# Turned modulation product, a projection that opens tile by tile, and other PSUM banks for attention's output

## The reference

```python
shift, scale, gate = jnp.split(jax.nn.silu(c) @ ada_w[l] + ada_b[l], 3, axis=-1)
shift_c, scale_c, gate_c = jnp.split(jax.nn.silu(c_ctx) @ ada_w[l] + ada_b[l], 3, axis=-1)
u = rms_norm(x, norm_w[l]) * (1.0 + scale[:, None, :]) + shift[:, None, :]
uc = rms_norm(ctx, norm_w[l]) * (1.0 + scale_c) + shift_c
rkv, ga, lw, la, q, k, v, gr, ma, mb = split_cols(u @ w_in[l])
...
# second block: causal attention with two softmaxes per head
a = p[:, :, 0] - lam * p[:, :, 1]
return jnp.einsum('bhqk,bhkv->bhqv', a.astype(vt.dtype), vt)
...
attn = rms_norm_2(attn, subln_w[l]) * (1.0 - lambda_init)
```

## Time and profile before

| | us |
|---|---|
| median of 3 runs | 5221.07 |
| profiled execution | 5224.11 |
| its span | 5222.3 |
| TensorE busy | 4907.5 (94%) |
| VectorE busy | 2560.6 (49%) |
| ScalarE busy | 1869.5 (36%) |
| GpSimd busy | 438.1 (8%) |
| mean granted clock of TensorE, share of 2.4 GHz | 0.959 |

### The profile page before, as it was taken

The page is one execution under the profiler, slowest core; times in us unless marked ns, Lnnn a source line. Parts: engine busy times, 40 slices in busy tenths (PEclk is TensorE's granted clock), DMA queues, the critical chain, the costliest instruction groups (busy, mean ns, idle before and its releaser), DMA issues. The chain is left out here.

```text
span 5222.3 us, 69250 instructions
## 1 busy us (share of the span) xinstructions
PE 4907.5 (94%) x29122; PEld 3966.2 (76%) x29122; DVE 2560.6 (49%) x3695; ACT 1869.5 (36%) x3141; POOL 438.1 (8%) x352
## 2 busy tenths in 40 slices
PE   8999999999989999999999779789999869999999
PEld 7878777778878888888888634367778547888777
DVE  2144545446434555555455367444543655555543
ACT  2133434345334554545455323311233653111111
POOL 0000000000012222232222100000000000000000
PEclk6999999999989999999999889889999879999999
DMA  4234333334221011011100153242220021212222
GB/s 174 86 131 146 130 137 140 131 140 148 104 104 44 13 49 52 13 57 44 57 13 1 50 157 116 73 139 96 97 76 30 17 89 65 73 73 73 81 93 89
DMA packets 149364, 444.05 MB, mean 85 GB/s; under 512 B 16432, under 2 KB 46256, under 8 KB 131776
## 3 DMA queue, kind: packets, MB, share of 16 engines
q1 hardware_dynamic: 133712, 385.03, 21.0%
q0 software_dynamic: 9584, 33.63, 1.8%
q10 hardware_dynamic: 5760, 20.97, 1.1%
HBM read 295.91 MB, written 142.61 MB: 84 GB/s over the span
## 5 line engine op out<-in xcount | busy, mean ns | idle before, releaser
L167 PE MATMUL pr_ps<-uhl,w_split 128*128 128x512 f32 (+1 forms) x1520 | 589.3, 388 | 0.7 <-PEq L198 0.7
L171 PE MATMUL pr_ps<-uhl,w_split 128*128 128x512 f32 (+1 forms) x1520 | 572.8, 377 | 0.0
L170 PE MATMUL pr_ps<-uhl,w_split 128*128 128x512 f32 (+1 forms) x1520 | 572.5, 377 | 0.0
L1349 DVE TENSOR_TENSOR b_G<-b_ps,cst 128x512 fp32r<-128x512 f32 x480 | 328.4, 691 | 335.5 <-PE b_ps L1150 334.2
L132 ACT ACTIVATE w_split<-w_ring 128x2048 fp32r<-128x2048 f32 x112 | 214.1, 1911 | 750.5 <-DVE ou_vc L2962 271.2
L167 PEld LDWEIGHTS pr_ps<-uhl,w_split 128*128 128x128 f32 x1520 | 288.3, 190 | 79.7 <-issue 29.3
L170 PEld LDWEIGHTS pr_ps<-uhl,w_split 128*128 128x128 f32 x1520 | 288.2, 190 | 56.9 <-issue 6.3
L171 PEld LDWEIGHTS pr_ps<-uhl,w_split 128*128 128x128 f32 x1520 | 287.9, 189 | 53.2
L1030 ACT ACTIVATE b_X<-b_ps 128x512 fp32r<-128x512 f32 x400 | 240.0, 600 | 242.0 <-PE b_ps L1150 242.0
L1150 PE MATMUL b_ps<-b_G,b_Y 128*128 128x128 f32 x1920 | 313.3, 286 | 13.5 <-DVE b_G L1349 13.1
L1034 ACT ACTIVATE b_Y<-b_ps 128x512 fp32r<-128x512 f32 x480 | 286.6, 597 | 88.6 <-PE b_ps L1150 88.6
(11 more groups left out here) (444 smaller groups left out, 10156.5 us busy)
## 6 DMA issues: line engine op xcount, KB each, us to landing
w_ring<-in_w_in SPq DMA_DIRECT2D x49, 1024.0 KB, 5.2
proj<-pr_stage SPq DMA_DIRECT2D x160, 256.0 KB, 2.0
w_ring<-in_w_up SPq DMA_DIRECT2D x24, 1024.0 KB, 4.7
ar<-pr_AR SPq DMA_DIRECT2D x32, 512.0 KB, 2.7
b_AR<-ar SPq DMA_DIRECT2D x16, 1024.0 KB, 8.8
pr_raw<-proj SPq DMA_DIRECT2D x48, 256.5 KB, 3.5
ada<-in_ada_w SPq DMA_DIRECT2D x24, 512.0 KB, 3.5
ff<-ou_vc ACTq DMA_DIRECT2D x24, 512.0 KB, 2.6
```

The costliest lines, as they stand in the source:

```text
L167: mm = nc.tensor.matmul(dst, a[0], b[0], start=start, stop=False)
L170: nc.tensor.matmul(dst, a[0], b[1], start=False, stop=False)
L171: return nc.tensor.matmul(dst, a[1], b[0], start=False, stop=stop)
L1349: L[x]["dve"].done(V.tensor_tensor(Gs[x][:], heads(x, 0), rep(K(f"lev{m}"), 4), ALU.mult), f"{n}.G{m}")
```

## The change

- The modulation product is turned: `cond` is the stationary operand, padded with zeros from 2 to 32 columns, and the weights are the moving one. Two matmuls of 512 columns per slab (column groups 0 and 1, or 2 and 3, by turns) for the first 16 slabs, four of 256 columns (groups 0 to 3) for the last 8. ScalarE copies the resulting rows out of PSUM (`line`), TensorE turns them with 4 and 2 transposes, and VectorE adds the bias. `ada_w` is laid out by rows; a slab stays 512 KB.
- Each square is done in two halves of 640 tokens in four banks.
- Weight chunk 1 is loaded behind all slabs and the constants, and the identity matrix ahead of the slabs; the others of the constants are waited for in `project`.
- The first block ends with three tiles of `uhl` made (`CUT_EARLY`); the other five are made at the start of `project`. The first six jobs become `opening`, which loops over k outside and over the jobs inside, and waits for each tile of `uhl`.
- `project` allocates the same tensors in another order, so that the ones over the old place of `u` are written late.
- In attention, heads 0 and 1 are flipped at t = 0 of heads 2 and 3, head 2 at the end before the last product, through banks 1 and 3; head 3 last, through banks 4 and 5. `end` is two instructions. `gates` waits for `head_out`.

The diff, cut:

```diff
+CUT_EARLY = 3
...
+class Modulate:
...
+    def scale(self, k):
+        for a, lo, hi in ((0, 0, T), (1, T, TA)):
+            ins = self.nc.vector.tensor_scalar(self.u[:, k, lo:hi], self.u[:, k, lo:hi], self.mod[:, 8 + k, a:a + 1],
+                                               self.mod[:, k, a:a + 1], ALU.mult, ALU.add)
+        ins.then_inc(self.ready, 1)
+
+    def hi(self, act, k):
+        act.wait_ge(self.ready, k + 1)
+        self.cut.hi(self.hl, k, self.u[:, k])
+
+    def lo(self, dve, k, base):
+        dve.wait_ge(self.cut.hi_ready, base + k + 1)
+        self.nc.vector.tensor_tensor(self.hl[1][:, k], self.u[:, k], self.hl[0][:, k].bitcast(F32), ALU.subtract).then_inc(self.cut.lo_ready, 1)
...
+    MS, MT, CA, SP, SQ = 16, 24, 2 * HALF, TA // 2, TA // 4
...
-        cond = sb("cond", [P, KT, 2])
...
+        cond = sb("cond", [P, KT, 32])
...
-        aw = sb("ada", [P, NA, KT, P])
-        ps = ctx.enter_context(nc.psum_tensor("ps_norm", [P, 4, HALF], F32))
+        aw = sb("ada", [P, NA, CA])
+        line = sb("ada_row", [P, 3 * CH])
+        ps = ctx.enter_context(nc.psum_tensor("ps_norm", [P, 8, HALF], F32))
@@ -205,14 +231,14 @@
                 sp.dma_start(par[:], G["par_dram"]).then_inc(par_in, 16)
                 for k in range(KT):
                     sp.dma_start(u[:, k], xT[:, k]).then_inc(x_in[k], 16)
+                sp.dma_start(ident, G["cst_dram"][:, CST["ident"] * P:(CST["ident"] + 1) * P]).then_inc(ident_in, 16)
                 for m in range(MS):
                     load_ada(m)
-                for l in range(NBUF):
-                    ring.load(sp, w_first[l], 0, 0, l, split=True)
+                ring.load(sp, w_first[0], 0, 0, 0, split=True)
                 for m in range(MS, MT):
                     load_ada(m)
-                sp.dma_start(G["cst"][:], G["cst_dram"]).then_inc(cst_in, 16)
-                sp.wait_ge(cst_in, 16)
+                sp.dma_start(cst[:, P:], G["cst_dram"][:, P:]).then_inc(G["cst_in"], 16)
+                ring.load(sp, w_first[1], 0, 0, 1, split=True)
 
@@ -224,19 +250,23 @@
...
-                    if k:
-                        act.wait_ge(sq_summed, k)
-                    nc.scalar.activation(sq[:], u[:, k], ACT.Square).then_inc(sq_ready, 1)
-                act.wait_ge(sq_summed, KT)
+                    for h in range(2):
+                        if k:
+                            act.wait_ge(sq_summed, 2 * k + h - 1)
+                        nc.scalar.activation(sq[:, h * SP:(h + 1) * SP], u[:, k, h * SP:(h + 1) * SP], ACT.Square).then_inc(sq_ready, 1)
+                act.wait_ge(sq_summed, 2 * KT)
...
+                act.wait_ge(ada_used, MS)
+                nc.scalar.activation(line[:, 0:HALF], ps[:, 4], ACT.Copy).then_inc(line_out, 1)
                 ring.split_first(act, True)
-                for k in range(KT):
-                    act.wait_ge(u_ready, 2 * k + 2)
-                    cut.hi([uhl[:, 0], uhl[:, 1]], k, u[:, k])
+                for k in range(CUT_EARLY):
+                    mdl.hi(act, k)
+                act.wait_ge(ada_used, MT)
+                nc.scalar.activation(line[:, HALF:], ps[:, 5, 0:CH], ACT.Copy).then_inc(line_out, 1)
@@ -244,65 +274,71 @@
...
-                    pe.wait_ge(sq_ready, k + 1)
-                    for c in range(3):
-                        w = min(HALF, TA - c * HALF)
-                        mm = nc.tensor.matmul(ps[:, c, 0:w], ones[:], sq[:, c * HALF:c * HALF + w],
-                                              start=k == 0, stop=k == KT - 1)
-                    mm.then_inc(sq_summed, 1)
-                pe.wait_ge(cond_ready, 1)
...
-                for m in range(MT):
+                    for h in range(2):
+                        pe.wait_ge(sq_ready, 2 * k + h + 1)
+                        for b in (2 * h, 2 * h + 1):
+                            mm = nc.tensor.matmul(ps[:, b, 0:SQ], ones[:], sq[:, b * SQ:(b + 1) * SQ], start=k == 0, stop=k == KT - 1)
+                        mm.then_inc(sq_summed, 1)
+                pe.wait_ge(cond_ready, 2)
+
+                def ada(m, bank, groups, w, k):
                     pe.wait_ge(ada_in[m % NA], 16 * (m // NA + 1))
-                    for k in range(KT):
-                        mm = nc.tensor.matmul(ps[:, 3, 2 * m:2 * m + 2], aw[:, m % NA, k], cond[:, k, :], start=k == 0, stop=k == KT - 1)
+                    for n, g in enumerate(groups):
+                        mm = nc.tensor.matmul(ps[32 * g:32 * g + 32, bank, 0:w], cond[:, k], aw[:, m % NA, n * w:(n + 1) * w], start=k == 0, stop=k == KT - 1)
                     mm.then_inc(ada_used, 1)
-                    if m == MS - 1:
-                        pe.wait_ge(u_ready, 1)
+
+                def turn(tiles, bank, at, n):
+                    pe.wait_ge(line_out, n)
+                    for j in range(tiles):
+                        mm = nc.tensor.transpose(ps[:, bank, j * P:(j + 1) * P], line[:, at + j * P:at + (j + 1) * P], ident)
+                    mm.then_inc(turned, 1)
+                for m in range(MS):
+                    ada(m, 4, (0, 1) if m % 2 == 0 else (2, 3), HALF, m // 2)
+                pe.wait_ge(ident_in, 16)
+                turn(4, 6, 0, 1)
+                for m in range(MS, MT):
+                    ada(m, 5, range(4), CH, m - MS)
+                turn(2, 7, HALF, 2)
...
+                nc.vector.memset(cond[:], 0.0).then_inc(cond_ready, 1)
...
-                ring.split_first(dve, False)
...
-                def row(m0, m1):
+                def row(m0, tiles, bank, n):
+                    m1 = m0 + 4 * tiles
+                    dve.wait_ge(turned, n)
...
+                row(0, 4, 6, 1)
...
-
-                def modulate(k):
-                    for a, lo, hi in ((0, 0, T), (1, T, TA)):
-                        nc.vector.tensor_scalar(u[:, k, lo:hi], u[:, k, lo:hi], mod[:, 8 + k, a:a + 1],
-                                                mod[:, k, a:a + 1], ALU.mult, ALU.add).then_inc(u_ready, 1)
-                modulate(0)
-                for k in range(KT):
-                    if k + 1 < KT:
-                        modulate(k + 1)
-                    cut.lo(dve, [uhl[:, 0], uhl[:, 1]], k, u[:, k])
-                dve.wait_ge(ada_used, MT)
-                row(MS, MT)
+                mdl.scale(0)
+                ring.split_first(dve, False)
+                for k in range(CUT_EARLY):
+                    mdl.scale(k + 1)
+                    mdl.lo(dve, k, 0)
+                row(MS, 2, 7, 2)
                 s.wait()
-                cut.wait(dve, KT)
-        cut.base += KT
+        G["cut"].base += KT
@@ -486,6 +523,7 @@
 
             @block.gpsimd
             def _(pool):
+                mdl.cut.wait(pool, 0)
@@ -506,6 +544,17 @@
...
+                def opening():
+                    for k in range(KT):
+                        mdl.cut.wait(pe, k + 1 - KT)
+                        for j in range(NB):
+                            l, m, c, w = jobs[j]
+                            rows = slice(m * P, (m + 1) * P)
+                            mm = product3(nc, ps[:, j, 0:w], [h[:, k, rows] for h in hl], [uhl[:, e, k, c:c + w] for e in range(2)],
+                                          k == 0, k == KT - 1, begun if j == 0 and k == 0 else None)
+                            if k == KT - 1:
+                                mm.then_inc(made, 1)
@@ -522,6 +571,7 @@
...
+                            pe.wait_ge(G["cst_in"], 16)
...
-                    dense(j)
+                    if j == 0:
+                        opening()
+                    elif j >= NB:
+                        dense(j)
@@ -628,6 +681,8 @@
...
+                for k in range(CUT_EARLY, KT):
+                    mdl.hi(act, k)
@@ -747,6 +802,11 @@
...
+                for k in range(CUT_EARLY, KT):
+                    if k + 1 < KT:
+                        mdl.scale(k + 1)
+                    mdl.lo(dve, k, mdl.cut.base - KT)
+                dve.wait_ge(G["cst_in"], 16)
@@ -2305,6 +2365,7 @@
...
+        flat_at = lambda h, x: ps[:, 4 + x] if h + 1 == A_HEADS else ps[:, 1 + 2 * x]
@@ -2349,8 +2410,6 @@
...
-                    if t == 5 and h:
-                        pe.wait_ge(head_out, h)
@@ -2369,6 +2428,8 @@
                 def gates(k, x):
                     if x == 0:
                         pe.wait_ge(conv, k + 1)
+                        if k >= 2:
+                            pe.wait_ge(head_out, k - 1)
@@ -2382,7 +2443,7 @@
                 def flip(h):
                     pe.wait_ge(scaled, h + 1)
                     for t in range(8):
-                        mm = nc.tensor.transpose(TR[:, t * P:(t + 1) * P], raw[:, h % 2, t], K("ident"))
+                        mm = nc.tensor.transpose(flat_at(h, t // 4)[:, t % 4 * P:(t % 4 + 1) * P], raw[:, h % 2, t], K("ident"))
@@ -2391,15 +2452,17 @@
...
-                    if t == 6 and h:
-                        pe.wait_ge(aT_ready, n - 1)
-                        flip(h - 1)
```

(24 more changed lines are left out.)

32 lines of the change are left out of this document (18 added, 14 removed).

## The result

The changed kernel takes **5162.5 us** (median of 4 runs, 5158.6 to 5163.6); the kernel before, timed beside it, 5221.9 us (5217.6 to 5230.3, 4 runs). The ratio is 0.9883, with a 95% interval of 0.9866 to 0.9900: 59 us or 1.2% faster. The forecast was 5150 with a range of 5132 to 5175. The profiled execution has a span of 5159.7 us (before: 5222.3), 62.6 us shorter.

A forecast was written before the change was run, and what follows sets the result against it. The prediction took TensorE to bound the span nearly everywhere; 54.3 us from the first stage plus 16.5 from attention make 70.8 off the median 5221.1, so 5150 us, range 5132 to 5175.

The forecast's parts named there:

- The squares: First stage: half squares of 640 columns make TensorE the bound; end moves from 38.1 to near 27.0 us.
- "low clock" of the first tile: First stage, squares: the first tile stays at 4.61 us, put down to a low clock.
- The price of a slab: Modulation product: column groups run side by side; 1.00 us of TensorE per early slab, at most 0.5 to 1.0 per late.
- The rivals that live from TensorE as the bound: Modulation product costs TensorE more than transfers: opening at 70 to 162, time 5158 to 5250; chances 0.13, 0.07, 0.04, 0.03.
- (b): Modulation product: column groups don't run side by side, at the high clock; opening at 77, time 5165; chance 0.07.
- (a): Modulation product: clock stays low while slabs stream, 2.0 us each; opening at about 70, time 5158; chance 0.13.
- The pace of the slabs: Modulation product: weights pace it at 1.35 us per slab, bounds 1.26 and 1.6; projection opens at about 62.0.
- The new wait before job 6: End of the projection's opening: TensorE waits 2.2 us, as ScalarE and VectorE split chunk 1 after job 0.
- First stage: Up to the projection's job 6: opening 56.5 us earlier less a new wait of 2.2, giving 54.3 us.
- Attention: Attention: other banks remove three waits for ScalarE's evacuation; net 18.8 - 0.6 - 1.9 = 16.3, taken as 16.5 us.
- The 5.8 for the clock in head 2: Attention, unit 7 to next unit 0: long wait lowered the clock; distance falls from 12.30 to 6.47, gaining 5.8 us.
- What is late next is VectorE's `p` for unit 5: Attention: with the three waits for ScalarE gone, VectorE's `p` comes next; unit 6 to 7 takes head 0's 10.94 us.

## Why the prediction was right, and where not

**The squares** were forecast to end at 27.0 and ended at 26.0. Right; what is late next was hidden, as said. The forecast's "low clock" of the first tile was an inference from 4.61 us where the other tiles take 2.42: the granted clock reads 1.00 from 6 to 12 us, so what slowed that tile isn't shown.

**The price of a slab** was 1.00 us of TensorE from a row with two groups. A slab alone took 1.05, so this was right; only where four lay ready and shared four groups were they 0.48 each. The rivals that live from TensorE as the bound fall. One group, the condition of (b), opened the projection at 69.0, not 77: a column cost 0.86 ns (0.44 us for 512) and not 0.95, and three of the slabs kept their groups. The clock was low for parts of this stage (0.83 and 0.66 in two of the stretches), as (a) feared. The fifth and sixth slab took 3.21 us together for that, and even then TensorE waited for the next one, so at most a little of the pace is due to it.

**The pace of the slabs** is the term that failed. Forecast were 1.35 us, a fifth slab at 31.6, the twenty-fourth used at 60.2. The fifth came at 30.65, but from there to the last it was 33.1 us for 19 slabs and the chunk: with 2.5 for the chunk, 1.61 us a slab, the forecast's upper bound. The round trip was put together from a landing time of 3.5 us of a lone slab; with four under way the median is 5.3. The forecast treated the 415 GB/s and the round trip as two limits of which the larger counts; with four buffers each cost some. The projection opened at 66.95 instead of 62.0; that the fifth slab came 0.9 us early was lost again behind the last one. And the pause from 22 to 28 us was in the forecast's own words, "four slabs are in place when the squares end", without the step that the queue stands still meanwhile. The run with ten buffers shows both.

**The new wait before job 6** was forecast at 2.2 us and measured 2.2 (2.17). The rounds of the opening waited for nothing and took 3.48 us, the first, at the low clock, 5.62. First stage: 49.3 instead of 54.3, the whole miss being the pace.

**Attention**: the mechanism held and half the sum did not. From unit 6 to 7, 4.78 + 4.78 + 3.45 = 13.0 were forecast; measured are 4.2 + 4.2 + 4.45 = 12.9. The 5.8 for the clock in head 2 were not won (12.10 from unit 7 to the next 0, where 12.30 stood), and head 1 lost 5.3 there (12.30 for 7.03). The step that failed is the argument that the long wait had brought the clock down and a short one would not. In head 1 the clock fell inside the new wait of 3.9 us, where behind the old one of 7.3 it was soon back. In head 2 it fell before the wait had begun. With the waits filled it fell in neither. The 8.1 us measured are 12.9 less 5.3, plus and minus small terms. "What is late next is VectorE's `p` for unit 5" was right, and the row of what VectorE itself was waiting for there, which the forecast did not read, held another 23 us, the clock's share included.

**The unchanged stages** were taken as unchanged. In the profiled pair they gave 5.3 us (55.9 less 49.3 before attention, then 1.3 lost), which brings the span to -62.6. That part is luck. It is no effect of the change. The mixing stage, with the same instructions, takes 642.1 us before, 636.6 after, and 642.1 in the second run of the kernel after. The mean clock was 0.98, 0.99 and 0.98. The row of the kernel before (columns as in the earlier trace rows):

```profile
3409.00:4051.10 642.10, 624.38 (x2775) 495.94 (x2776) 288.54 (x300) 160.47 (x142) 24.57 (x49) 0.98 0.24 82
```

The row of the kernel after in its second run:

```profile
3360.40:4002.50 642.10, 624.39 (x2775) 495.82 (x2776) 288.55 (x300) 160.48 (x142) 24.57 (x49) 0.98 0.24 82
```

Without it, 49.3 + 8.1 = 57.4, and the medians say 59.

So the time was inside the range and 12.5 us above the forecast: 5.0 from the slabs' pace, 8.4 from attention, less what the unchanged stages happened to give (5.3 us in the profiled pair, some 2 in the medians).

## What to carry to other kernels

When a wait goes, read on the engine that is late next not only how long it works but what it waits for itself: in attention a step of 1.2 us, queued ahead of what TensorE needed, held more than the banks did. A stream through few buffers pays twice, once while the consumer is busy elsewhere and once because each landing takes longer than alone; memory that is written only later can lend the buffers. A stage in which nothing was edited can differ by 5 us from one kernel to the next, so a difference of a few us is to be read at fixed points of the program, and not from the total.

## What the runs showed of the hardware

- Matmuls with 32 output columns each, in different column groups over all 128 rows, run side by side: 16 passes of 512 columns in four groups in 1.92 us (0.12 each), 48 such passes in one group in 21.11 us (0.44 each). Groups 2 and 3 work like 0 and 1.
- The DMA engines can read 92 to 98% busy and move 325 to 350 GB/s with four transfers of 512 KB under way, and 412 to 414 GB/s with ten (share 1.02 and 1.03); the busy share hardly tells the two apart.
- Behind waits of TensorE of 3.9 and 3.1 us in heads 1 and 2 the passes ran at the 1.2 GHz level, and the next distance was 5 us longer in each. In head 2 the granted clock was at 0.50 before the wait began. Eight matmuls that nobody reads, in each head's wait, removed both stretches and made the kernel 9 us faster.
- Leads of 1.6 to 1.8 us at the start of the projection held for some 350 us and then, within 130 us, shrank to 0.4 or grew to 4.4, as the mean clock of those 130 us was 0.97, 0.99 or 1.00 from kernel to kernel.
